# Two slabs' tiles modulated ahead of the next rows, first weights in the slabs' queue, sample outputs with q stationary

## What is computed

```
mod = c_act @ w_ada[i] + b_ada[i]
sh1, sc1, gt1, sh2, sc2, gt2, sh3, sc3, gt3 = jnp.split(mod, N_ADA, axis=-1)
h = modulate(rms_norm(x, norm_ffn1[i]), sh1, sc1)      # h * (1 + scale) + shift
x = x + 0.5 * gt1[:, None, :] * swiglu(h, ffn1_gate[i], ffn1_up[i], ffn1_down[i])
...
s_new = exp(b_last) * s + k^T v                          # GLA state, per head 128 x 256
o = q s_new                                              # per sample token
```

## Time and profile before

| | us |
|---|---|
| runs, median of 3 | 1575.96 (1571.41 to 1578.43) |
| profiled execution, device time | 1576.69 |
| its span in the profile | 1574.7 |
| TensorE busy | 1466.4 (93%) |
| VectorE busy | 823.6 (52%) |
| ScalarE busy | 485.1 (31%) |
| GpSimd's small constants (`sel`, `eps`) end | 6.4 |
| ScalarE's root, which first waits for them | 14.70 |
| w_lo (L1280), mean of 218 | 1.22 |

### The profile page before, as it was taken

How to read it: one execution, slowest core, us unless ns; L and a number is a source line. 1 busy time by engine, 2 the same in 40 slices (tenths; PEclk the granted TensorE clock), 3 DMA queues, 4 the chain that set the end, 5 groups by cost and what they waited for, 6 DMA issues and landing times. The chain is left out here.

```text
span 1574.7 us, 30308 instructions
## 1 busy us (share of the span) xinstructions
PE 1466.4 (93%) x11966; PEld 1417.7 (90%) x11966; DVE 823.6 (52%) x1381; ACT 485.1 (31%) x652; POOL 69.9 (4%) x103
## 2 busy tenths in 40 slices
PE   4899999999998998899998998799979999999996
PEld 3799999999997998899898897699979999999995
DVE  3332323232337485698965968775463333333345
ACT  4322222222235221524231333622252212222233
POOL 5000000000001000000000000000000000000000
PEclk8899999999999998999998998799989999999997
DMA  9355454545446223132333243242213232232311
GB/s 320 129 173 186 135 187 133 186 136 186 133 160 212 81 80 111 54 108 64 109 124 120 88 138 137 77 144 96 81 61 100 80 102 86 84 103 81 100 60 54
DMA packets 135044, 189.03 MB, mean 120 GB/s; under 512 B 3515, under 2 KB 115535, under 8 KB 134926
## 3 DMA queue, kind: packets, MB, share of 16 engines
q1 hardware_dynamic: 114476, 115.62, 23.2%
q0 software_dynamic: 16432, 63.70, 12.0%
q10 hardware_dynamic: 4050, 8.53, 1.4%
HBM read 174.37 MB, written 14.41 MB: 120 GB/s over the span
## 5 line engine op out<-in xcount | busy, mean ns | idle before, releaser
L1280 DVE TENSOR_TENSOR w_lo<-raw,w_hi 128x1024 fp32r<-128x1024 f32 x218 | 266.7, 1224 | 603.7 <-ACT w_hi L931 603.5
L531 PE MATMUL pu<-h_hi,w_hi 128*128 128x260 f32 x2480 | 510.2, 287 | 22.1 <-DVE w_lo L1280 12.4
L531 PE MATMUL pu<-h_hi,w_lo 128*128 128x260 f32 x2480 | 503.1, 285 | 0.0
L531 PE MATMUL pu<-h_lo,w_hi 128*128 128x260 f32 x2480 | 503.0, 285 | 0.0
L931 ACT CAST w_hi<-raw 128x1024 fp32r<-128x1024 f32 x218 | 228.1, 1047 | 694.1 <-PE pu L531 674.6
L531 PEld LDWEIGHTS pu<-h_hi,w_hi 128*128 128x128 f32 x2480 | 386.6, 191 | 30.1 <-DVE w_lo L1280 13.1
L531 PEld LDWEIGHTS pu<-h_lo,w_hi 128*128 128x128 f32 x2480 | 386.5, 191 | 0.0
L531 PEld LDWEIGHTS pu<-h_hi,w_lo 128*128 128x128 f32 x2480 | 386.3, 190 | 0.0
L1569 DVE SCALAR_TENSOR_TENSOR d<-u,cw,d 128x512 f32<-128x512 f32 x240 | 162.8, 743 | 0.0
L531 PE MATMUL pu<-f_hi,w_hi 128*128 128x260 f32 x704 | 143.0, 284 | 2.0 <-DVE f_lo L1523 2.0
L531 PE MATMUL pu<-f_hi,w_lo 128*128 128x260 f32 x704 | 141.8, 283 | 0.0
(11 more groups left out here) (250 smaller groups left out, 1275.2 us busy)
## 6 DMA issues: line engine op xcount, KB each, us to landing
raw_a<-in_w_ada POOLq DMA_DIRECT2D x32, 1024.0 KB, 7.8
raw<-in_w_in SPq DMA_DIRECT2D x30, 1024.0 KB, 5.3
raw<-in_ffn_gate SPq DMA_DIRECT2D x22, 1024.0 KB, 5.3
raw<-in_ffn_up SPq DMA_DIRECT2D x22, 1024.0 KB, 5.3
raw<-in_ffn_down SPq DMA_DIRECT2D x16, 1024.0 KB, 5.1
raw_a<-in_w_ada_final POOLq DMA_DIRECT2D x8, 1024.0 KB, 7.2
gates_d<-sg ACTq DMA_DIRECT2D x24, 260.0 KB, 2.1
raw<-in_ffn_down SPq DMA_DIRECT2D x8, 768.0 KB, 4.5
```

Of the source, the lines that this page charges most:

```text
L531: last = mm(pu[p][:, e, 0:HALF], w[p][:, k, :], m[:, k, e * HALF:(e + 1) * HALF], start=(k == 0 and j == 0), stop=(k == k_tiles - 1 and j ...
L1280: V.tensor_tensor(w_lo[p][:], raw[:, slot, :, p * P:(p + 1) * P], w_hi[p][:].bitcast(F32), ALU.subtract).then_inc(s_lo, 1)
```

## The change

Three things. (1) In the opening, `modulate` and `first_tiles` are dissolved: for each two slabs, ScalarE copies the rows, then modulates both tiles, then casts both; only then come the rows of the next two slabs. VectorE normalizes two tiles ahead (`first_normed`), does the scale, the samples (`first_samples`) and the splits (`first_split`). A new semaphore tells ScalarE when the scale is there. (2) The first weight slab leaves SP's program and stands third in GpSimd's, behind slabs 0 and 1; loads 1 to 5 move ahead of `sel` and `eps`; both its halves are cast after the rows of slabs 0 and 1. (3) `sample_o` becomes two steps: `q8` (8 query columns, zeros to 32) stationary and the states moving, in four column groups, ahead of the last two grams; a ScalarE copy of the 128 x 512 result into `E_[:, 1]`; and four products with a selecting matrix `sel_o` that take and transpose the wanted rows. GpSimd makes `sel_o` and `q8`, four more instructions behind the masks.

```
-            first_load(0)
+            for i in range(2):
+                first_load(i)
+            wv = A["ffn1_gate"][0].rearrange("(k p) n -> p k n", p=P)
+            pool.dma_start(raw[:, 0], wv[:, :, 0:256]).then_inc(s_w0, 16)
+            for i in range(2, 6):
+                first_load(i)
...
+            nc.gpsimd.memset(sel_o[:], 0.0).then_inc(s_const, 1)
+            nc.gpsimd.memset(q8[:], 0.0).then_inc(s_const, 1)
+            pool.wait_ge(s_const, n + 3)
+            for r in range(2):
+                nc.gpsimd.affine_select(out=sel_o[:, r, :], in_=sel_o[:, r, :], compare_op=ALU.not_equal, fill=1.0,
+                                        base=-4 * r, pattern=[[-CG - 1, 4]], channel_multiplier=1).then_inc(s_const, 1)
...
+            def sample_o_rows(h):
+
+                pe.wait_ge(s_sn, h.value(8, 8))
+                pe.wait_ge(s_q8, h.value(1, 1))
+                for b in range(NS):
+                    g, r = b % 4, b // 4
+                    last = mm(pg[CG * g:CG * (g + 1), 2, r * DV:(r + 1) * DV], q8[:], ST[:, b, :],
+                              start=True, stop=True, tile_position=(0, CG * g))
+                last.then_inc(s_qo, 1)
+
             def sample_o(h):
-                pe.wait_ge(s_sn, h.value(8, 8))
-                q = tile(qk, h.value(2))
+
+                pe.wait_ge(s_qr, h.value(1, 1))
                 for t in range(2):
-                    for b in range(NS):
-                        last = mm(pg[:, 2, t * NS + b:t * NS + b + 1], ST[:, b, t * P:(t + 1) * P],
-                                  q[:, NP + b:NP + b + 1], start=True, stop=True)
+                    for r in range(2):
+                        last = mm(pg[:, 3, t * NS + 4 * r:t * NS + 4 * r + 4],
+                                  E_[:, 1, r * DV + t * P:r * DV + (t + 1) * P], sel_o[:, r, :], start=True, stop=True)
                 last.then_inc(s_o, 1)
...
                         if s == 5:
+                            sample_o_rows(h)
                             gram(h, 6)
                             gram(h, 7, tile(qk, h.value(2)))
                             sample_o(h)
...
+            for t in range(0, KT, 2):
                 first_rows(t)
                 first_rows(t + 1)
+                if t == 0:
+                    split_hi(Lin(0), 0, 0)
+                    split_hi(Lin(1), 1, 0)
+                act.wait_ge(s_scale, t // 2 + 1)
+                for k in (t, t + 1):
+                    act.wait_ge(s_xn, k + 1)
+                    full = sg[:, k % 2, 0:NP]
+                    af(full, full, ACT.Identity, bias=mod[:, 8 * SH1 + k, 0:1], scale=mod[:, 8 * SC1 + k, 0:1]
+                       ).then_inc(s_hf, 1)
+                for k in (t, t + 1):
+                    act.wait_ge(s_hf, k + 1)
+                    nc.scalar.copy(h_hi[:, k, 0:NP], sg[:, k % 2, 0:NP]).then_inc(s_hh, 1)
...
+                            af(q8[:, 0:NS], tile(qk, h.value(2), NP, N), ACT.Copy).then_inc(s_q8, 1)
...
                         if s == 5:
+                            act.wait_ge(s_qo, h.value(1, 1))
+                            act.wait_ge(s_gm, h.value(10, MIX[6]))
+                            nc.scalar.copy(E_[:, 1, :], pg[:, 2, :]).then_inc(s_qr, 1)
...
+            first_normed(0)
+            for t in range(0, KT, 2):
                 first_out(t)
                 first_out(t + 1)
+                first_samples(t)
+                if t == 0:
+                    split_lo(Lin(0), 0, 0)
+                    split_lo(Lin(1), 1, 0)
+                first_split(t)
+                if t + 2 < KT:
+                    first_normed(t + 2)
```

More of the change, by code:

```diff
@@ L57 @@
 LN_EXP, SILU, SIGMOID, EXP_TANH = "natural_log_exp_and_others", "silu_and_others", "sigmoid_and_others", "exp_and_others"
-CONSTS = 32
+CONSTS = 36
 CONSTS_START = 3
@@ L219, in decoder_step @@
         sel = sb("sel", [P, 10])
+        sel_o = sb("sel_o", [P, 2, 4])
+        q8 = sb("q8", [P, CG])
         eps = sb("eps", [P, 1])
@@ L263, in sems @@
             return {k: sem(v) for k, v in names.items()}
-        s_raw = [sem("raw0_loaded"), sem("raw1_loaded")]
+        s_w0, s_raw = sem("first_raw_loaded"), [sem("raw0_loaded"), sem("raw1_loaded")]
         s_free = sem("raw_slabs_found_free")
@@ L280, in decoder_step @@
         s_ar, s_at, s_mod = sem("ada_rows_ready"), sem("ada_rows_transposed"), sem("modulation_ready")
+        s_scale = sem("first_scales_ready")
         s_sq, s_sqf, s_ss = sem("square_ready"), sem("square_added"), sem("sums_in_psum")
@@ L344, in load @@
             def load(n, slot, src, k=KT):
+                if n.i is None and n.base == 0:
+                    return
                 if n.i is not None or n.base >= 4:
@@ L434, in _ @@
             nc.gpsimd.memset(eps[:], EPS).then_inc(s_const, 1)
-            for i in range(1, 8):
+            for i in range(6, 8):
                 first_load(i)
@@ L928, in split_hi @@
             def split_hi(n, p, slot):
-                act.wait_ge(s_raw[slot], n.half().half().value(16, 16))
+                if n.i is None and n.base < 2:
+                    act.wait_ge(s_w0, 16)
+                else:
+                    act.wait_ge(s_raw[slot], n.half().half().value(16, 16 * slot))
                 nc.scalar.copy(w_hi[p][:], raw[:, slot, :, p * P:(p + 1) * P]).then_inc(s_hi, 1)
@@ L1019, in _ @@
             first_copy(6)
-            split_hi(Lin(0), 0, 0)
-            first_rows(0)
-            first_rows(1)
-            split_hi(Lin(1), 1, 0)
-            first_rows(2)
-            first_rows(3)
-            modulate(0, SC1, SH1, range(0, 2))
-            for t in range(4, KT, 2):
+            for t in range(0, KT, 2):
                 first_rows(t)
                 first_rows(t + 1)
-                modulate(0, SC1, SH1, range(t - 2, t))
-            modulate(0, SC1, SH1, range(KT - 2, KT))
+                if t == 0:
[10 more added lines that the diff above has]
+                    nc.scalar.copy(h_hi[:, k, 0:NP], sg[:, k % 2, 0:NP]).then_inc(s_hh, 1)
             def ffn(which):
@@ L1199, in _ @@
                         if s == 5:
+                            act.wait_ge(s_qo, h.value(1, 1))
+                            act.wait_ge(s_gm, h.value(10, MIX[6]))
+                            nc.scalar.copy(E_[:, 1, :], pg[:, 2, :]).then_inc(s_qr, 1)
                             dst = qk[:, bass.ds(h.value(2), 2), :]
                             act.wait_ge(s_o, h.value(2, 1))
-                            nc.scalar.copy(dst[:, :, NP:N], pg[:, 2, 0:2 * NS].rearrange("p (t b) -> p t b", t=2)
+                            act.sem_inc(s_os8, 1)
+                            nc.scalar.copy(dst[:, :, NP:N], pg[:, 3, 0:2 * NS].rearrange("p (t b) -> p t b", t=2)
                                            ).then_inc(s_oe, 1)
@@ L1276, in split_lo @@
             def split_lo(n, p, slot):
-                dve.wait_ge(s_raw[slot], n.half().half().value(16, 16))
+                if n.i is None and n.base < 2:
+                    dve.wait_ge(s_w0, 16)
+                else:
+                    dve.wait_ge(s_raw[slot], n.half().half().value(16, 16 * slot))
                 dve.wait_ge(s_hi, n.value(1, 1))
@@ L1309, in first_out @@
                     gain = vt[:, VROW["norm_ffn1"] + i - 1:VROW["norm_ffn1"] + i + 1].unsqueeze(2).to_broadcast([P, 2, 10])
-                    chain.link(V.scalar_tensor_tensor(sc, sc, 1.0, gain, ALU.add, ALU.mult))
+                    V.scalar_tensor_tensor(sc, sc, 1.0, gain, ALU.add, ALU.mult).then_inc(s_scale, 1)
+                    dve.wait_ge(s_scale, i // 2 + 1)
             def ada_out(m):
@@ L1361, in rstd, with first_normed @@
                 refine_d(sg[:, 3, :], ps[:, 0:2, 0:HALF]).then_inc(s_rstd, 1)
-            def first_tiles(t):
+            def first_normed(t):
                 for k in (t, t + 1):
@@ L1368, in first_tiles, with first_samples @@
                     V.tensor_tensor(sg[:, k % 2, 0:NP], x[:, k, 0:NP], sg[:, 3, 0:NP], ALU.mult).then_inc(s_xn, 1)
+            def first_samples(t):
                 two = slice(t, t + 2)
@@ L1375, in first_tiles, with first_split @@
                 V.tensor_tensor(h_lo[:, two, NP:N], hs[:, two, :], h_hi[:, two, NP:N].bitcast(F32), ALU.subtract)
+            def first_split(t):
                 for k in (t, t + 1):
@@ L1484, in _ @@
             dve.wait_ge(s_rstd, 1)
-            split_lo(Lin(0), 0, 0)
-            first_out(0)
-            first_out(1)
-            split_lo(Lin(1), 1, 0)
-            first_out(2)
-            first_out(3)
-            first_tiles(0)
-            for t in range(4, KT, 2):
+            first_normed(0)
+            for t in range(0, KT, 2):
                 first_out(t)
                 first_out(t + 1)
-                first_tiles(t - 2)
-            first_tiles(KT - 2)
+                first_samples(t)
[5 more added lines that the diff above has]
+                    first_normed(t + 2)
             dve.wait_ge(s_tp, 4 + KT)
```

3 lines of the change are left out of this document (2 added, 1 removed).

## The result

| | before | after |
|---|---|---|
| runs, median | 1576.26 (1571.41 to 1578.43, 4 runs) | 1553.03 (1552.37 to 1553.64, 4 runs) |
| ratio | 1 | 0.9862, 95% interval 0.9844 to 0.9880 |
| profiled execution, its span | 1576.69, 1574.7 | 1552.72, 1551.1 |
| unit 2 starts | 72.38 | 53.19 |
| mean granted clock of TensorE | 0.957 | 0.966 |

The change gains 23.2 us. The forecast was 15.8. The time lies 0.03 us inside the low end of the range (1553), and two of its four runs (1552.37 and 1552.72) lie outside. Of the 23.6 us between the two spans, 19.2 are gained before unit 2 (72.38 - 53.19) and 4.4 behind it, where 0.2 had been forecast.

What follows compares the result with a forecast made beforehand. TensorE was taken to bound the kernel behind an opening with time to give. From 1576.69, 15.6 us for the opening and 0.2 for the heads gave 1560.9, stated as 1560.5 after adjusting to the runs' median; range 1553 to 1570.

Steps and rivals of the forecast that it cites:

- The bound, and what passes on: Whole kernel: TensorE bounds it behind the opening, so time the opening gives is passed on one for one.
- The start of the pair: Opening: with earlier weights and the new order, the pair's first tile starts at 29.1 us, not 39.28.
- The pair: Opening's tiles: waits shrink to about 1 us, the clock rises once, and the pair ends at about 48.8, not 70.52.
- GpSimd late: Opening: masks slowed beside VectorE (81% loss) end at 45, slabs 8 and 9 land late, unit 2 starts at 55.1.
- rival 1: Opening: GpSimd on time, masks end by 41, unit 2 at 51.6; 20 to 22 us gained, 1555.5; chance 0.22.
- The clock behind the start: At unit 2's start: TensorE, idle over 4 of 6 us, falls to half clock and pays 1.7 us (0 to 3.4).
- The heads: Four heads' ends: removed sample products turn into waits for VectorE's merges; 0.2 us gained, bounds -0.4 and +7.
- Behind the opening: After unit 2's start: only the heads' 0.2 us gain was forecast.
- The sum: Whole kernel: 1576.69 - 15.6 - 0.2 = 1560.9, stated as 1560.5; forecast's chance 0.46.
- Rival 2: Opening: the clock stays at half through the pair, unit 2 at 63.4; 9 us gained, 1567.5; chance 0.17.
- Rival 3: Opening: selects and VectorE hold each other up, deciding from a last constant at 62.3; slower, 1582; chance 0.04.
- Rival 4: Opening: GpSimd's queued loads lose their order, first weights land near 32, start at 38.6; 11 us, 1566; chance 0.06.

Runs made afterwards that it cites:

- e11_after_again: The kernel after, unaltered, timed and profiled once more: 1553.51 us, ratio 0.9858 to the kernel before.
- e5_masks_late: Kernel after with GpSimd's masks and new constants moved behind the loads of slabs 8 and 9: 1556.14 us, ratio 0.9883 to the kernel before.
- e3_heads: Kernel before with only the new sample outputs, plus GpSimd's four new instructions and the new semaphores: 1572.06 us, ratio 0.9963.
- e6_masks_long: Kernel after with 40 more selects at the end of GpSimd's masks, result unchanged: 1569.64 us, ratio 0.9969 to the kernel before.

## Why the prediction was right, and where its sizes were off

**The bound, and what passes on.** Right: what the opening gives is passed on, and nothing behind it grew by more than it shrank.

**The start of the pair.** Forecast 29.1, measured 30.33. The order, the first weights without a wait and the casts came as worked out. The miss is in the loads: each slab landed 0.7 to 1.4 us later than I had counted back (slab 2 at 23.4 and slab 3 at 26.6, not 22.1 and 25.4; slab 6 at 36.4, not 35.3). TensorE waits 2.08 us for slab 3. The timeline names ScalarE's copy of slab 2's rows, which ends at 26.74, 0.1 us behind the landing; in e11_after_again the same wait is put down to the load:

```profile
26.86 1.60 PE L581 MATMUL pg<-work,c_f 128*32 128x256 f32 x16 [2.11 <-DMA work<-in_w_ada]
```

And the product runs at half clock, 1.94 us instead of 1.07, as do the transposes, 1.88 instead of 1.2.

**The pair.** 19.7 us from the first tile to its end forecast (29.1 to 48.8), 19.7 measured (30.33 to 50.05): the clock rises once, four slabs with transposes take 2.95 a pair (2.9), two tiles 3.0.

**GpSimd late.** This step failed. I took the last constant at 45: 37.3 without contention, and most of 81% of VectorE's work with two SBUF operands on top. It came at 38.8, and the loads went at 42.4, when the buffers came free, as in rival 1 (41). The row was read rightly: the select had lost 0.63 us, since its pair takes 1.36 and not 1.99 beside an idle VectorE. What failed is what I made of it. First, the masks before had lost 1.9 us and not 0.6, so without contention the chain would end near 35.6 (an estimate: 22.92 + 12.1 + 0.6 for the new constants) and not at 37.3. Second, the masks then lost 3.2 us, where I had put 7.7. VectorE's work on two SBUF operands lay beside the selects for about 9 us, so that is some 35% and not 81%. The 81% is that of a select that began while `w_lo` was running; the one that had begun before `w_lo` kept its 0.65, with `w_lo` beside it for 0.44 us. Slab 9 was then ready at 52.19, not 54.1. With the pair's end 1.2 later, unit 2 began at 53.19 instead of 55.1: 1.9 us more gain.

The Trainium skill, "SBUF — State Buffer", section "Who interferes with whom", says that such a VectorE instruction contends with a GpSimd instruction that reads SBUF, and calls contention an exclusive lock; that it lasts for a whole instruction the page says of VectorE's two-port modes, and I had taken it over. The traces agree that both sides lose: GpSimd 3.2 us, and VectorE 1.9, which is busy 12.1 us between 22.9 and 38.3 here and 10.2 in e5_masks_late, with 28 operations in both. They don't agree with an exclusion for as long as both are at work, since these 5.1 us are less than the 9; and the select that had begun first held `w_lo` back by no more than 0.06 us.

**The clock behind the start.** I charged 1.7 us for a fall as at 49.9. TensorE's idle time was 1.07 us, not 4, and the clock held. The kernel after, at the wait and behind it:

```profile
50.05:53.19 3.14, 2.07 (x33) 0.92 (x33) 1.23 (x1) 1.32 (x3) 0.88 (x1) 1.00 0.12 42
53.19:60.00 6.81, 6.81 (x61) 6.81 (x58) 1.23 (x1) 2.59 (x4) 0.88 (x1) 1.00 0.96 317
```

**The heads.** Durations and waits came as worked out: 1.07 for 1.0, 1.05 for 0.9, waits of 1.07 to 3.35 for 2 to 3. The removed products turned into waiting, too: in e3_heads TensorE's idle time rose by 6.5 us (108.3 to 114.8), and 4 x (3.73 - 1.07 - 1.05) = 6.4 had been removed. The term was forecast at 0.2 and measured at 2.9 on top of the opening, 3.6 to 8.0 alone. What failed is the sign of the clock. My bounds were a gain of 0.4 and a loss of 7, for a clock that falls earlier in each head; that it might get better stood in neither, and both measured gains lie outside. In e3_heads the mean clock is 0.960 instead of 0.957, and TensorE's busy time fell by 8.5 us, 2.1 more than was removed. Three successive stretches, from 810.3 to 936.6 in times of before, differ by -1.81, +0.67 and -1.69 us. Whether the products that were removed, or the places of the waits that came for them, made the clock better stays open: no run changed the one without the other.

By the Trainium skill, "TensorEngine Tiling (Array Packing)", section "Key Properties", each switch of mode drains TensorE. In the head's rows above the next full products (L811) start 1.00 us behind the start of the column-grouped ones, which last 1.07, so no gap is seen; the first eight records behind the switch take 1.16 us and the next eight 1.06, so a drain is worth 0.1 us at most.

**Behind the opening.** Nothing but the 0.2 was forecast, 4.4 us came in the profile, of which the heads explain 2.9. The rest, 1.5 us, is within what the clock does from one profile to the next (4.4 and 2.5 for the same kernel), and it stays open which earlier work decides that.

**The sum.** 15.8 forecast, and 1.9 (GpSimd on time, less the late start), 1.7 (no fall of the clock) and 4.2 (behind the opening) more: 23.6, the difference of the spans. That the time is inside the range is in part luck: the late loads did not happen, the clock did not fall behind them and the heads gave what no term held, and all three made the kernel faster, to 0.03 us of the range's end. What happened at GpSimd is rival 1, to which I had given 0.22; it worked out 1555.5, and the time is 2.5 below it. Rival 2 (half clock through the pair) fell with the row at 33.08. Rival 3 fell with the masks' end at 38.8, though its threshold was real, as e6_masks_long shows. Rival 4 fell with ScalarE's cast at 22.02, which waited for no DMA.

## What to carry to other kernels

In a chain of engines, let each engine finish the step that the bound engine needs next before it takes rows for a later one: by medians the order alone gave 15 us of the 21, the earlier load alone 3. Before one instruction's loss is taken as a rate of contention, look at the others beside it: which of the two engines began first, and how long the chain takes with none at all. When work is taken off the bound engine at a meeting point, look at who is next there and move its slack work behind the meeting in the same step; here that second edit was worth 11 us, more than the first. And look at the bound engine's busy time before a gain is put down to shorter waits.

## What the runs showed of the chip

- GpSimd's selects of one shape (128 x 128 bf16) took from 0.69 to 3.33 us a pair with VectorE all but idle, by the level of the mask, and each pair that can be seen so in two kernels the same within 0.01 us; forty equal ones that wait for each other came 0.48 apart.
- Beside VectorE's operations of two SBUF inputs a select that began second took 0.63 us longer, and one that began first kept its 0.65; VectorE's went from 1.29 to as much as 1.86 us a pair. Over the chain GpSimd lost 3.2 and VectorE 1.9 of 9 us in which both were at work.
- Equal work with equal waits (3 of 5 us idle) was run at a clock of 1.00 in one kernel and fell to 0.54 in the other, while the total time of eight executions stayed within 1.6 us.
- With 5.9 us less of waiting at the heads' ends TensorE's idle time fell by 1.9 us and its busy time by 10.1, for the same records, with the mean clock up from 0.965 to 0.973.
